# Feed-forward part: own counters for the down products, no drains around the first group, two weight units split ahead of the loop

## The reference

```python
def _conv_ffn(x, w_up, conv_w, conv_b, w_down):
    u = x @ w_up                                   # 1024 -> 2 * 2816
    u = sum(conv_w[CONV_WIDTH - 1 - j] * _shift(u, j) for j in range(CONV_WIDTH)) + conv_b
    gate, val = jnp.split(u, 2, axis=-1)
    return (jax.nn.silu(gate) * val) @ w_down      # 2816 -> 1024
...
        h = _layer_norm(DEEPNORM_ALPHA * h + mixed @ w_out[l], ln1_g[l], ln1_b[l])
        f = _conv_ffn(h, w_up[l], conv_w[l], conv_b[l], w_down[l])
        h = _layer_norm(DEEPNORM_ALPHA * h + f, ln2_g[l], ln2_b[l])
```

## Time and profile before

| what | value |
|---|---|
| median of 3 runs | 4340.82 us (4338.72 to 4342.36) |
| the profiled execution | 4342.19 us |
| its span, first to last instruction | 4340.4 us |
| TensorE matmuls busy | 88% of the span |
| VectorE, ScalarE, GpSimd busy | 48%, 25%, 22% |
| mean granted TensorE clock | 0.943 of full |
| feed-forward part of layer 1, from gB0 to the last down product | 1351 to 2142 us |
| of layer 2 | 3470 to 4261 us and on to 4264 |

### The profile page before, as it was taken

The page is one execution under the profiler, slowest core; times in us unless marked ns, Lnnn a source line. Parts: engine busy times, 40 slices in busy tenths (PEclk is TensorE's granted clock), DMA queues, the critical chain, the costliest instruction groups (busy, mean ns, idle before and its releaser), DMA issues. The chain is left out here.

```text
span 4340.4 us, 67687 instructions
## 1 busy us (share of the span) xinstructions
PE 3825.1 (88%) x28223; PEld 3490.0 (80%) x28223; DVE 2076.1 (48%) x2468; ACT 1072.3 (25%) x1510; POOL 934.1 (22%) x460
## 2 busy tenths in 40 slices
PE   4888989898886999999978889898988789999995
PEld 4655988886885999999864579797868689999994
DVE  2144346565445444444522444574635534444456
ACT  3245124222004111111222530441221221212122
POOL 3000310000332333333210014000023223333330
PEclk9988999999998999999988899998998899999998
DMA  4321235422410111111024102552223011111111
GB/s 105 89 65 31 73 120 185 120 73 60 135 39 25 44 45 44 49 45 43 29 66 110 50 30 88 163 167 82 70 89 101 29 35 45 44 47 46 44 44 49
DMA packets 372475, 305.79 MB, mean 70 GB/s; under 512 B 118199, under 2 KB 325651, under 8 KB 372227
## 3 DMA queue, kind: packets, MB, share of 16 engines
q1 hardware_dynamic: 333668, 244.07, 19.9%
q10 hardware_dynamic: 38559, 58.12, 3.9%
HBM read 219.87 MB, written 82.26 MB: 70 GB/s over the span
## 5 line engine op out<-in xcount | busy, mean ns | idle before, releaser
L196 PE MATMUL psum<-h_hi,w_hi 128*128 128x348 f32 x3792 | 823.1, 326 | 128.8 <-DVEq L2170 49.0
L227 POOL TENSOR_TENSOR w_hi<-w_raw,consts 128x1024 fp32r<-128x1024 f32 (+1 forms) x206 | 377.1, 1831 | 2072.5 <-PE psum L196 1936.5
L196 PE MATMUL psum<-h_lo,w_hi 128*128 128x348 f32 x3792 | 816.3, 324 | 1.8 <-issue 1.8
L196 PE MATMUL psum<-h_hi,w_lo 128*128 128x348 f32 x3792 | 812.2, 323 | 0.0
L196 PEld LDWEIGHTS psum<-h_hi,w_hi 128*128 128x128 f32 x3792 | 645.5, 190 | 136.8 <-issue 57.2
L196 PEld LDWEIGHTS psum<-h_lo,w_hi 128*128 128x128 f32 x3792 | 649.7, 190 | 2.3 <-issue 2.3
L196 PEld LDWEIGHTS psum<-h_hi,w_lo 128*128 128x128 f32 x3792 | 643.0, 189 | 0.0
L229 POOL TENSOR_TENSOR w_lo<-w_raw,w_hi 128x1024 fp32r<-128x1024 f32 (+1 forms) x206 | 499.6, 2425 | 16.1
L2397 DVE SCALAR_TENSOR_TENSOR cv_g<-up_g,cw,cv_g 128x1044 f32<-128x1044 f32 x44 | 137.7, 3130 | 333.5 <-ACT cv_g L2324 333.5
L2397 DVE SCALAR_TENSOR_TENSOR cv_v<-up_v,cw,cv_v 128x1044 f32<-128x1044 f32 x44 | 146.8, 3337 | 302.2 <-ACT cv_v L2324 302.2
L2379 DVE TENSOR_TENSOR acc<-acc,psum 128x1044 f32<-128x1044 f32 x176 | 217.8, 1238 | 144.9 <-PE psum L196 141.6
(11 more groups left out here) (270 smaller groups left out, 5350.7 us busy)
## 6 DMA issues: line engine op xcount, KB each, us to landing
w_raw<-in_w_up SPq DMA_DIRECT2D x88, 512.0 KB, 3.8
w_raw<-in_w_in SPq DMA_DIRECT2D x70, 512.0 KB, 5.0
w_raw<-in_w_down SPq DMA_DIRECT2D x44, 512.0 KB, 3.5
gate_scratch<-gst ACTq DMA_DIRECT2D x32, 522.0 KB, 3.0
gbuf<-gate_scratch SPq DMA_DIRECT2D x32, 522.0 KB, 3.5
prep_scratch<-prep ACTq DMA_DIRECT2D x8, 2080.0 KB, 8.6
pc<-prep_scratch SPq DMA_DIRECT2D x20, 832.0 KB, 4.5
rkv_scratch<-mixed_p ACTq DMA_DIRECT2D x24, 522.0 KB, 4.2
```

Source lines behind the costliest of these rows:

```text
L196: last = nc.tensor.matmul(bank[:, n, :], w(k), x(k)[:, nrange(n)], start=(k == 0 and q == 0), stop=(k == kt - 1 and q == 2))
L227: nc.gpsimd.tensor_tensor(w_hi[s][:, 0:width], w_raw[s][:, 0:width], consts[:, 4:5].broadcast_to([P, width]), ALU.mult).then_inc(hi_done.s ...
```

## The change

Up and down steps get counters of their own: `pdn` on TensorE and `ddn` on VectorE count the down products and their adds, and `pes` and `dves` the rest. Each is moved to its first value by one `give` or `start_at` at the head of its engine's queue. `skip` and all its drains are gone. TensorE's A products get a wait for ScalarE's copy (before, the counter passed by the drain stood for it). GpSimd splits units 0 to 5 ahead of its loop, the first two as soon as the output projection is through with the slot (the second also after c0), and the loop's twelve units are shifted by two. `Phase` makes sure that the semaphores of a phase have consecutive numbers.

```diff
@@ Phase.__enter__
         self.sems = [self.stack.enter_context(self.nc.semaphore(n)) for n in self.names]
+        gap = [i for i in range(1, len(self.sems)) if self.sems[i].num != self.sems[i - 1].num + 1]
+        if gap:
+            more = [self.stack.enter_context(self.nc.semaphore(f"more_{n}")) for n in self.names[:gap[0]]]
+            self.sems = self.sems[gap[0]:] + more
@@ names
-            pe_n += [f"{x_}{B}{i}" for i in range(FG) for x_ in "gv"] + [f"d{B}{m}" for m in range(KD)]
+            pe_n += [f"{x_}{B}{i}" for i in range(FG) for x_ in "gv"]
...
-                steps = [f"{n}{B}{i}" for n in ("t1g", "t0g", "t1v", "t0v", "f", "lo")]
-                if i == FG - 1:
-                    steps[3:3], steps[5:5], steps[7:7] = [f"d{B}0"], [f"d{B}1"], [f"d{B}2"]
-                dve_n += steps
-            dve_n += [f"d{B}{m}" for m in range(3, KD)]
+                dve_n += [f"{n}{B}{i}" for n in ("t1g", "t0g", "t1v", "t0v", "f", "lo")]
+        dn_n = [f"d{B}{m}" for B in "AB" for m in range(KD)]
...
+            pdn, ddn = Steps(sm[27], dn_n), Steps(sm[28], dn_n)
@@ skip
-            def skip(me, eng, first):
-
-                n = (me.names.index(first) if first else me.per) - me.at
-                if n > 0:
-                    eng.drain().then_inc(me.sem, n)
-                me.at = (me.at + n) % me.per
@@ GpSimd
-                def free(i, s):
-
-                    return (pes.sem, pes.of(i, unit_step[s - 2])) if s >= 2 else (pes.sem, pes.of(i, unit_step[s - 2], 1))
+                def free(i, name):
+
+                    done = pdn if name[0] == "d" else pes
+                    return done.sem, done.of(i, name)
...
-                for s in range(UP):
-                    if s < 2:
-                        pool.wait_ge(o_used.sem, o_used.of(KD - 1 + s))
-                    if s == 1:
+                for u in range(UP + 2):
+                    if u == 1:
                         pool.wait_ge(n1.dve.sem, n1.dve.of(0, "c0"))
-                    split_unit(pool, s, s % 2, s // 2 + 1, loaded, hi_done, split, free(-1, NU // 2 + s))
+                    split_unit(pool, u, u % 2, u // 2 + 1, loaded, hi_done, split,
+                               free(-1, unit_step[NU // 2 + u - 2]) if u >= 2 else (o_used.sem, o_used.of(KD - 1 + u)))
                 with pool.Fori(0, NP) as i:
                     for s in range(NU):
-                        split_unit(pool, i * NU + (UP + s), s % 2, i * (NU // 2) + ((UP + s) // 2 + 1), loaded, hi_done, split, free(i, s))
-                for s in range(2):
-                    u = NP * NU + UP + s
-                    split_unit(pool, u, s, u // 2 + 1, loaded, hi_done, split, free(NP, s))
+                        split_unit(pool, i * NU + (UP + 2 + s), s % 2, i * (NU // 2) + ((UP + 2 + s) // 2 + 1), loaded, hi_done, split, free(i, unit_step[s]))
@@ TensorE, up_products
                         elif B == "B":
-                            pe.wait_ge(dves.sem, dves.of(i, f"dA{KD - 2 + s}"))
+                            pe.wait_ge(ddn.sem, ddn.of(i, f"dA{KD - 2 + s}"))
                         else:
-                            pe.wait_ge(dves.sem, dves.of(i, f"dB{KD - 2 + s}", 1))
+                            pe.wait_ge(acts.sem, acts.of(i, f"c{x_}B{FG - 1}", 1))
+                            pe.wait_ge(ddn.sem, ddn.of(i, f"dB{KD - 2 + s}", 1))
@@ TensorE
+                start_at(pes, pe, "gB0")
+                pdn.give(pe)
...
                 norm_pe(pe, n1)
-                start_at(pes, pe, "gB0")
                 up_products(-1, "B", 0)
-                skip(pes, pe, None)
...
-                skip(pes, pe, "dA0")
                 down_products(NP, "A", NP * NU + UP, None)
@@ ScalarE
+                start_at(acts, act, "rgB0")
                 n1.act.give(act)
...
-                start_at(acts, act, "rgB0")
@@ VectorE
+                start_at(dves, dve, "cwB")
+                ddn.give(dve)
...
                 norm_dve(dve, n1)
-                start_at(dves, dve, "cwB")
...
                     if isinstance(i, int) and i < 0:
-                        at = dves.names.index(f"d{B}{m}")
-                        skip(dves, dve, dves.names[at + 1])
                         return
...
                 up_tiles(-1, "B", 0)
-                skip(dves, dve, None)
...
                 for m in range(KD):
-                    if dves.names[dves.at] != f"dA{m}":
-                        skip(dves, dve, f"dA{m}")
                     down_tile(NP, "A", m)
```

More of the change, by code:

```diff
@@ L2142, in layer @@
             for i in range(FG):
-                steps = [f"{n}{B}{i}" for n in ("t1g", "t0g", "t1v", "t0v", "f", "lo")]
-                if i == FG - 1:
-                    steps[3:3], steps[5:5], steps[7:7] = [f"d{B}0"], [f"d{B}1"], [f"d{B}2"]
-                dve_n += steps
-            dve_n += [f"d{B}{m}" for m in range(3, KD)]
+                dve_n += [f"{n}{B}{i}" for n in ("t1g", "t0g", "t1v", "t0v", "f", "lo")]
+        dn_n = [f"d{B}{m}" for B in "AB" for m in range(KD)]
         with Phase(nc, "o_raw0_loaded", "o_raw1_loaded", "o_hi_done", "o_split", "o_used", "o_steps", "n1_pe", "n1_act", "n1_dve",
                    "raw0_loaded", "raw1_loaded", "hi_done", "split", "used", "pe_steps", "act_steps", "dve_steps", "pads", "tot_zero",
-                   "n2_pe", "n2_act", "n2_dve", "next0_in", "next1_in", "next_hi", "next_lo", "ab_done") as (block, sm):
+                   "n2_pe", "n2_act", "n2_dve", "next0_in", "next1_in", "next_hi", "next_lo", "ab_done", "pe_down", "dve_down") as (block, sm):
             o_loaded, o_hi_done, o_split, o_used = stream(sm[0:5])
@@ L2263, in down_products @@
                             else:
-                                pe.wait_ge(dves.sem, dves.of(i, f"dB{KD - 2 + m}", 1))
+                                pe.wait_ge(ddn.sem, ddn.of(i, f"dB{KD - 2 + m}", 1))
                             if B == "A":
@@ L2270, in down_products @@
                         else:
-                            pe.wait_ge(dves.sem, dves.of(i, f"d{B}{m - 2}"))
-                        pes.did(product(pset[m % 2], FG, wtile(w_hi[s], FG, 512, (m % 4) * P), wtile(w_lo[s], FG, 512, (m % 4) * P), hk(f_hi[par]), hk(f_lo[par])), f"d{B}{m}")
+                            pe.wait_ge(ddn.sem, ddn.of(i, f"d{B}{m - 2}"))
+                        pdn.did(product(pset[m % 2], FG, wtile(w_hi[s], FG, 512, (m % 4) * P), wtile(w_lo[s], FG, 512, (m % 4) * P), hk(f_hi[par]), hk(f_lo[par])), f"d{B}{m}")
+                start_at(pes, pe, "gB0")
+                pdn.give(pe)
                 def tile_ready(k):
@@ L2330, in up_tiles @@
                         if B == "A":
-                            act.wait_ge(pes.sem, pes.of(i, f"dB{KD - 1}", 1))
+                            act.wait_ge(pdn.sem, pdn.of(i, f"dB{KD - 1}", 1))
                         else:
-                            act.wait_ge(pes.sem, pes.of(i, f"dA{KD - 1}"))
+                            act.wait_ge(pdn.sem, pdn.of(i, f"dA{KD - 1}"))
                         acts.did(nc.scalar.activation(f_hi[0 if B == "B" else 1][:, p_, :], cv["v", p_][:, :], ACT.Copy), f"hi{B}{p_}")
@@ L2340, in _ @@
                     act.wait_ge(next_in[s], 16)
-                    act.wait_ge(pes.sem, pes.of(NP, f"dA{4 * s + 3}"))
+                    act.wait_ge(pdn.sem, pdn.of(NP, f"dA{4 * s + 3}"))
                     nc.scalar.activation(w_hi[s][:, :], w_raw[s][:, :], ACT.Copy).then_inc(next_hi, 1)
@@ L2372, in down_tile @@
                     if isinstance(i, int) and i < 0:
-                        at = dves.names.index(f"d{B}{m}")
-                        skip(dves, dve, dves.names[at + 1])
                         return
-                    dve.wait_ge(pes.sem, pes.of(i, f"d{B}{m}"))
+                    dve.wait_ge(pdn.sem, pdn.of(i, f"d{B}{m}"))
                     if m == 0:
-                        dve.wait_ge(dves.sem, dves.of(i, f"dA{KD - 1}") if B == "B" else dves.of(i, f"dB{KD - 1}", 1))
-                    dves.did(nc.vector.tensor_tensor(chunks3(acc[:, m, :]), chunks3(acc[:, m, :]), pset[m % 2], ALU.add), f"d{B}{m}")
+                        dve.wait_ge(ddn.sem, ddn.of(i, f"dA{KD - 1}") if B == "B" else ddn.of(i, f"dB{KD - 1}", 1))
+                    ddn.did(nc.vector.tensor_tensor(chunks3(acc[:, m, :]), chunks3(acc[:, m, :]), pset[m % 2], ALU.add), f"d{B}{m}")
                 def up_tiles(i, B, g):
@@ L2428, in _ @@
                         continue
-                    dve.wait_ge(dves.sem, dves.of(NP, f"dA{m}"))
+                    dve.wait_ge(ddn.sem, ddn.of(NP, f"dA{m}"))
                     if m > 1:
```

## The result

The changed kernel took 4274.36 us (median of 4, 4271.02 to 4281.42) against 4341.59 for the kernel before in the same comparison: ratio 0.9844, with 95% confidence between 0.9824 and 0.9863. That is 67.2 us less. Two later comparisons gave 4282.36 against 4344.58 (0.9858, 0.9837 to 0.9878) and 4278.37 against 4343.91 (0.9858, 0.9838 to 0.9878), so 62.2 and 65.5 us less. The prediction had 4284.0 and a range from 4280 to 4299, which is 42 to 61 us less than the 4340.82 it started from. The direction and the mechanism of the two gaps held, and the size was too small: all three comparisons show a few us more than the range allowed, by 1 to 6 us.

The account below looks back on a forecast made before the run. TensorE, busy 88% of the span, bounds the kernel, with savings at the loop's entry. Per layer 12.0 + 15.9 + 0.5 = 28.4 us, two layers 56.8, giving 4284.0 us from the median 4340.82; range 4280 to 4299.

Parts of the forecast that it names:

- Gap 1: TensorE's wait between norm products and first up product, held by VectorE's down-add counter; 12.0 us per layer saved, 8.1 to 13.3.
- Rival (a): Clock: small pieces in the first gate product keep TensorE at 1.2 GHz; 8.1 not 12.0 us per layer, 4292; chance 0.08.
- Gap 2: TensorE's wait before the loop's first gate product: 14.18 us idle plus 1.73 clock climb, together 15.9 us per layer saved.
- The tail: TensorE's drain behind the loop, before the last down product, goes; 0.5 us per layer saved.
- The loop: 20 added TensorE waits for ScalarE's copies before the A products cost 0, bounds 0 or 1.04 us each.
- Rivals (b) to (f): Only gap 2 goes, 4308 (0.04); only gap 1, 4316 (0.03); issue gaps, 4286 (within 0.82); waits slow it (0.01); nothing (0.02).

## Why the prediction was right or wrong

**Gap 1** was forecast at 12.0 us per layer between 8.1 and 13.3, and was 13.0 and 13.3. The cause was right (putting the counter back gave back 19.4 us), and so was the removal of the split from VectorE's scaling steps. Mis-sized was the level of the clock: a value between the bounds was taken, and all but the first 5 us of the product ran at 1.00, as the upper bound had it. Rival (a) did not come: pauses of 0.4 to 0.75 us between bursts left the clock up. Longer pauses are not as safe: with the waits ahead of the loop, one of 2.5 us lowered the clock in one layer of two.

**Gap 2** was forecast at 15.9 us and was 14.2 + 1.7 = 15.9 in both layers, or 16.1 counted by starts. **The tail** was forecast at 0.5 and was 0.4.

**The loop** is the step that failed. The prediction wrote "Bounds: 0, or the 8.3 / 8 = 1.04 us of a wait that does end late; I take 0", with no bound below zero, and used the "issue" gaps only as a risk that the change might add one. It should have asked what they are: there were three in 600 us of a loop-bound stretch. The stops went from five to one between the two traces, 5.1 us. The best reading of the runs is that the two added waits make them rarer: with the waits alone, the kernel before had two stops twice in place of five to seven, and its times fell by 0.9 to 9 us. Why they do is open (two instructions more in the loop move its end, and they also change when TensorE's queue reaches the branch; no run separates the two), and with seven stops in one kernel that has them, chance isn't excluded. What is left of the difference between the first comparison and the later ones is the spread from run to run: the 1.5 us allowed for it were too little, as times of one kernel here lie up to 17 us apart in one comparison (before, 4332.98 to 4350.41). Much of it lies outside this part: between the two layers' feed-forward parts alone the traces differ by up to 6 us.

The sum by measured terms: 26.3 + 32.2 + 0.8 + 5.1 = 64.4 us, against 56.8 forecast and 62 to 67 measured. Also wrong was a name: the 211.6 us of the earlier trace rows, called one iteration, are one and a half (one without a stop is some 140 us). Nothing was worked out from it, but the gaps of the earlier trace rows were hence not recognised as sitting on loop-backs.

Rivals (b) to (f) are out: both gaps went, no wait for a split, a bank or VectorE's chain took their place, the 20 waits cost nothing, and the centring steps kept their 9.31 us.

## What to carry to other kernels

A counter that an engine moves past steps it never executes is a step in that engine's queue like any other: whoever waits for it waits for all that stands before it. Set such counters at the head of the queue, and give steps that are skipped a counter of their own. In a loop bound by one engine, look where its unexplained idle times sit; here they sat on the loop-back, where its code was fetched again, and edits that cost nothing of their own changed their number. If you shift code on purpose, count the instructions in the page: here two waits made one.

## What the runs showed of the hardware

A loop of about 1770 TensorE instructions came back without loading code in some iterations and with nine blocks of 16384 bytes loaded again in others, with a stop of 0.9 to 1.8 us in 92 cases of 96 and of 2.4 to 2.9 us in four. Each such reload in unshifted code began within about 1 us of the branch. Moved by 5, 10, 50 or 123 instructions, the code stopped at all eight loop-backs. Satisfied waits on TensorE stand two to an instruction, and these follow each other after 0.106 us. Bursts of 1.43 us in every 2.43 us kept its clock at the 2.4 GHz level once it was there. A single pause of 2.5 us behind steady work left it there in one layer and dropped it to the 1.2 GHz level for the next matmuls in the other, in both profiles of that kernel.
